# A reordered recurrence, a split output projection, and score rows masked by GpSimd in a two-block model kernel on one NeuronCore

## Time and profile before

| | us |
|---|---|
| median of 3 runs | 3749.43 (3748.31 to 3749.6) |
| profiled execution, its own time | 3750.95 |
| its span, first to last instruction | 3749.2 |
| PE busy | 3447.2 (92%) |
| POOL busy | 2500.9 (67%) |
| DVE busy | 1557.5 (42%) |
| ACT busy | 1491.3 (40%) |
| granted TensorE clock, mean | 0.941 of full speed |

### The profile page before, as it was taken

The page is one execution under the profiler, slowest core; times in us unless marked ns, Lnnn a source line. Parts: engine busy times, 40 slices in busy tenths (PEclk is TensorE's granted clock), DMA queues, the critical chain, the costliest instruction groups (busy, mean ns, idle before and its releaser), DMA issues.

```text
span 3749.2 us, 74946 instructions
## 1 busy us (share of the span) xinstructions
PE 3447.2 (92%) x29214; PEld 3340.4 (89%) x29214; DVE 1557.5 (42%) x2495; ACT 1491.3 (40%) x1968; POOL 2500.9 (67%) x1079
## 2 busy tenths in 40 slices
PE   7898878698999999978769899999999999999999
PEld 7877767598999999978659899999999999999999
DVE  1068543503222210046990158566660266116600
ACT  4345522234444433344333445434344333433333
POOL 5654510086888878855327678777778877877787
PEclk9988877699999999998879999999999999999999
DMA  5843310054556555543215455555556555555555
GB/s 175 187 131 105 102 34 2 24 170 145 181 183 182 182 168 185 185 131 120 83 57 158 143 159 180 168 168 157 171 164 186 175 173 166 182 176 172 171 168 168
DMA packets 158554, 556.41 MB, mean 148 GB/s; under 512 B 17457, under 2 KB 23793, under 8 KB 158305
## 3 DMA queue, kind: packets, MB, share of 16 engines
q1 hardware_dynamic: 151008, 540.08, 46.6%
q0 software_dynamic: 2704, 9.25, 1.4%
q10 hardware_dynamic: 4720, 5.36, 0.5%
HBM read 549.38 MB, written 5.24 MB: 148 GB/s over the span
## 4 chain that ended last, share of the span: by engine, by line
PE 80%; DVE 13%; issue 3%; ACT 2%; POOL 1%; DMA 1%; ACTq 0%; POOLq 0%; DVEq 0%; SPq 0%
PE ps L503 71%; DVE arena L1571 3%; PE ps L688 2%; PE ps L559 1%; PE ps L859 1%; POOL wl L447 1%; DVE arena L1347 1%; PE ps L520 1%; DVE arena L1540 1%; DVE arena L1344 1%; DMA raw<-w_qkv 1%; DVE misc L1538 1%; PE ps L713 1%; PE ps L714 1%; DVE arena L1433 0%
## 5 line engine op out<-in xcount | busy, mean ns | idle before, releaser
L447 POOL TENSOR_TENSOR wl<-raw,wh 128x1024 fp32r<-128x1024 f32 (+1 forms) x1034 | 2477.7, 2401 | 1142.8 <-ACT wh L933 1142.2
L933 ACT ACTIVATE wh<-raw 128x1024 fp32r<-128x1024 f32 (+1 forms) x1034 | 1086.8, 1053 | 1757.8 <-PE ps L503 1696.6
L503 PE MATMUL ps<-uh,wh 128*128 128x256 f32 x5584 | 1614.2, 289 | 83.5 <-DVE ul L1263 43.9
L503 PE MATMUL ps<-ul,wh 128*128 128x256 f32 x5584 | 1600.9, 287 | 0.0
L503 PE MATMUL ps<-uh,wl 128*128 128x256 f32 x5584 | 1598.9, 286 | 0.0
L503 PEld LDWEIGHTS ps<-uh,wh 128*128 128x128 f32 x5584 | 1093.8, 196 | 97.8 <-DVE ul L1263 45.5
L503 PEld LDWEIGHTS ps<-ul,wh 128*128 128x128 f32 x5584 | 1093.0, 196 | 0.4
L503 PEld LDWEIGHTS ps<-uh,wl 128*128 128x128 f32 x5584 | 1093.0, 196 | 0.0
L503 PE MATMUL ps<-el,wh 128*128 128x256 f32 x2048 | 577.5, 282 | 0.0
L503 PE MATMUL ps<-eh,wh 128*128 128x256 f32 x1536 | 439.3, 286 | 9.2 <-DVE el L1706 5.6
L503 PE MATMUL ps<-eh,wl 128*128 128x256 f32 x1536 | 430.3, 280 | 0.0
(11 more groups left out here) (313 smaller groups left out, 3165.0 us busy)
## 6 DMA issues: line engine op xcount, KB each, us to landing
raw<-w_u SPq DMA_DIRECT2D x256, 512.0 KB, 3.6
raw<-w_v SPq DMA_DIRECT2D x256, 512.0 KB, 3.6
raw<-w_gu SPq DMA_DIRECT2D x176, 512.0 KB, 3.6
raw<-w_down SPq DMA_DIRECT2D x80, 512.0 KB, 3.7
raw<-w_out SPq DMA_DIRECT2D x64, 512.0 KB, 3.7
raw<-w_z SPq DMA_DIRECT2D x54, 512.0 KB, 3.6
raw<-w_in SPq DMA_DIRECT2D x52, 512.0 KB, 3.6
raw<-w_qkv SPq DMA_DIRECT2D x48, 512.0 KB, 3.7
```

The lines of the kernel that those rows point to most:

```text
L447: pool.tensor_tensor(wl[:, slot, 0:width], raw[:, slot, 0:width], wh[:, slot, 0:width].bitcast(F32), ALU.subtract).then_inc(lo_ready, 1)
L503: ins = pe.matmul(out, w[:, slot, at], x(c), start=first and c == n == 0, stop=last and c == kt - 1 and n == 2)
L933: act.activation(wh[:, slot, 0:width], raw[:, slot, 0:width], ACT.Copy).then_inc(hi_ready, 1)
```

## The change

- z stage: ScalarE writes `(1 - mix) * z` straight to the destination, and VectorE adds `mix` times the PSUM tile shifted by one step, in place. `zraw`, `zdif` and the subtraction go; a bank is free once VectorE has read it.
- Recurrence: ScalarE copies the lower score rows from PSUM to QS, GpSimd multiplies them by the mask in SBUF. The state's part of y comes right after the right-hand side, the new state before u's part of y; waits are later and split.
- Output projection: first 16 units with the attention half as input, between the group-norm matmuls, each added to xT by `add_attention`; then 16 units with the other half. x is read in four DMAs in place of one. The mean of tile i comes ahead of unit MEAN_AT[i], and the variance of tile i-1 behind it.
- Convolution: the sums of even and odd taps are kept in PSUM bank 7.

`group_mean(i)` and `group_var(i)` hold the former mean and variance matmuls with the same waits.

```diff
+MEAN_AT = (0, 2, 3, 5, 6, 8, 10, 11)
+LAST_VAR_AT = 13
+HALF_BANKS = (2, 3, 6, 7)
...
-        zraw = view(arena, o, 2, T + 1); o += 2 * (T + 1)
-        zdif = view(arena, o, T); o += T
-        sc = view(arena, o, 12, T); o += 12 * T
+        RK = view(arena, o, 2, 2, T); o += 4 * T
+        sc = view(arena, o, 10, T); o += 10 * T
...
+        keep = small[:, 64:91]
+        def z_out(c):
+            i = c // 3 - 1
+            return lo[:, c, :] if c < 3 else vT[:, i, :] if c % 3 == 2 else RK[:, i % 2, c % 3, :]
...
-        odd_taps = qsc[:, 2, :]
+        even_taps, odd_taps = ps[:, 7, 0:T], ps[:, 7, T:2 * T]
...
+            def stream_half(name, dram, half):
+                base = BASE[name] + DT * half
+                with sp.Fori(0, DT // RING) as i:
+                    for j in range(RING):
+                        slot = (base + j) % RING
+                        sp.wait_ge(lo_ready, i * RING + (base + j - RING + 1))
+                        sp.dma_start(raw[:, slot, :],
+                                     dram[bass.ds(i * (2 * RING) + (2 * j + half), 1), :, :]
+                                     .rearrange("a p n -> p (a n)")).then_inc(w_in[slot], 16)
...
+                elif name == "out":
+                    stream_half(name, A["w_out"], 0)
+                    stream_half(name, A["w_out"], 1)
...
-            splits(BASE["out"], 32 + 176)
+            splits(BASE["out"], RING)
+            pool.wait_ge(lo_ready, BASE["out"] + RING)
+            for c in range(NC_):
+                for e in range(2):
+                    pool.wait_ge(low_copied, 2 * c + e + 1)
+                    part = QS.rearrange("p (k e) n -> p e k n", e=2)[CH:P, e, :, :]
+                    mask = cst("cmask")[CH:P].unsqueeze(1).to_broadcast([CH, 8, P])
+                    pool.tensor_tensor(part, part, mask, ALU.mult).then_inc(c_pool, 1)
+            pool.wait_ge(c_pool, 2 * NC_)
+            splits(BASE["out"] + RING, 32 - RING + 176)
...
-                        pe.wait_ge(z_raw, c - 1)
+                        pe.wait_ge(z_ready, c - 1)
...
+                for i in range(WT):
+                    ins = pe.transpose(bank(i // 4)[:, (i % 4) * P:(i % 4 + 1) * P], BK[:, i, c, :], ident)
+                ins.then_inc(bk_tr, 1)
                 if c:
-                    pe.wait_ge(y_ev, c)
-                    pe.wait_ge(st_ev, c)
-                for i in range(WT):
-                    pe.transpose(bank(i // 4)[:, (i % 4) * P:(i % 4 + 1) * P], BK[:, i, c, :], ident)
+                    pe.wait_ge(st_read, c)
...
                 for e in range(2):
                     hp = HD * e
+                    if c and e:
+                        pe.wait_ge(y_ev, c)
                     for k in range(8):
                         ins = pe.matmul(bank(4 + 2 * e + k // 4)[:, (k % 4) * P:(k % 4 + 1) * P],
                                         BK[hp:hp + HD, k, c, :], AR[hp:hp + HD, k, c, :], start=True, stop=True)
@@ -675,6 +712,7 @@
                 for n, step in enumerate(INVERSE):
                     if n == 0:
                         pe.wait_ge(c_dve, c + 1)
+                        pe.wait_ge(low_copied, 2 * c + 2)
...
+                if c:
+                    pe.wait_ge(st_ev, c)
+                pe.wait_ge(c_pool, 2 * c + 2)
...
+                y_out = lambda h: bank(6)[HD * (h % 2):HD * (h % 2) + HD, h // 2 * CH:(h // 2 + 1) * CH]
+                for h in range(NH):
+                    pe.matmul(y_out(h), SV[:, h, :], QS[:, h, CH:P], start=h < 2, stop=False, skip_group_check=True)
...
-                for g in range(GROUPS):
-                    pe.wait_ge(uv_ev, GROUPS * c + g + 1)
-                    for h in range(8 * g, 8 * g + 8):
-                        hp, k = HD * (h % 2), h // 2
-                        out = bank(6)[hp:hp + HD, k * CH:(k + 1) * CH]
-                        pe.matmul(out, SV[:, h, :], QS[:, h, CH:P], start=True, stop=False)
-                        ins = pe.matmul(out, UV[0:CH, h, :], MB[0:CH, h, CH:P], start=False, stop=True)
-                ins.then_inc(y_ps, 1)
+                pe.wait_ge(uv_ev, GROUPS * (c + 1))
                 for h in range(NH) if c < NC_ - 1 else ():
                     ins = pe.matmul(bank(2 + h // 8)[0:CH, (h % 8) * CH:(h % 8 + 1) * CH], BKn[:, h, :],
                                     UV[:, h, :], start=True, stop=True)
                 if c < NC_ - 1:
                     ins.then_inc(n_ps, 1)
-            for i in range(WT):
+                for h in range(NH):
+                    ins = pe.matmul(y_out(h), UV[0:CH, h, :], MB[0:CH, h, CH:P], start=False, stop=h >= NH - 2,
+                                    skip_group_check=True)
+                ins.then_inc(y_ps, 1)
...
-                if i:
-                    pe.wait_ge(gn_sq, i)
...
+            def group_var(i):
+                pe.wait_ge(gn_sq, i + 1)
+                if i >= 2:
+                    pe.wait_ge(gn_rc, i - 1)
+                pe.matmul(bank(4 + i % 2)[:, 0:T], blk, sc[:, i % 2, :], start=True, stop=True).then_inc(gn_var, 1)
+            for d in range(DT):
+                if d in MEAN_AT:
+                    i = MEAN_AT.index(d)
+                    group_mean(i)
+                    if i:
+                        group_var(i - 1)
+                if d == LAST_VAR_AT:
+                    group_var(WT - 1)
+                if d == 0:
+                    pe.wait_ge(ml_ready, 2)
+                if d >= len(HALF_BANKS):
+                    pe.wait_ge(res_attn, d - len(HALF_BANKS) + 1)
+                g = BASE["out"] + d
+                unit(bank(HALF_BANKS[d % 4])[:, 0:T], g + 1, g % RING, uhc, ulc).then_inc(w_used, 1)
+            pe.wait_ge(ml_ready, 2 + WT)
+            for d in range(DT):
+                if d >= 2:
+                    pe.wait_ge(res_ready, d - 1)
+                g = BASE["out"] + DT + d
+                unit(bank(d % 2)[:, 0:T], g + 1, g % RING, lambda c: uh[:, WT + c, :], lambda c: ul[:, WT + c, :])\
+                    .then_inc(w_used, 1)
...
-                    if c >= 2:
-                        act.wait_ge(z_ready, c - 1)
-                    else:
+                    if c == 0:
                         act.wait_ge(z_pad, 1)
-                    act.activation(zraw[:, c % 2, 1:T + 1], bank(c % 2)[:, 0:T], ACT.Copy).then_inc(z_raw, 1)
+                    if c >= 9 and c % 3 == 0:
+                        act.wait_ge(bo_used, c // 3 - 2)
+                    act.activation(z_out(c), bank(c % 2)[:, 0:T], ACT.Identity, scale=keep[:, c:c + 1])\
+                        .then_inc(z_raw, 1)
...
-                act.wait_ge(c_tr, c + 1)
+                act.wait_ge(bk_tr, c + 1)
...
+                for e in range(2):
+                    act.wait_ge(c_ps, 3 * c + e + 1)
+                    for b in range(2):
+                        src = bank(4 + 2 * e + b).rearrange("p (k n) -> p k n", k=4)
+                        ins = act.activation(QS4[CH:P, e, 4 * b:4 * b + 4, :], src[CH:P], ACT.Copy)
+                    ins.then_inc(low_copied, 1)
...
+                if c == NC_ - 1:
+                    act.wait_ge(v_ps, GROUPS * NC_)
+                    for k in (0, 4):
+                        act.activation(uh[:, k:k + 4, :], attnT[:, k:k + 4, :], ACT.Copy).then_inc(mh_ready, 1)
...
-            act.dma_start(xT[:, :, :], x_in).then_inc(s_x2, 16)
-            for c in (0, 4):
-                act.activation(uh[:, c:c + 4, :], attnT[:, c:c + 4, :], ACT.Copy).then_inc(mh_ready, 1)
+            for k in range(4):
+                act.dma_start(xT[:, 4 * k:4 * k + 4, :], x_in[:, 4 * k:4 * k + 4, :]).then_inc(s_x[k], 16)
...
+                for d in range(MEAN_AT[i], MEAN_AT[i + 1] if i + 1 < WT else LAST_VAR_AT):
+                    convert(BASE["out"] + d + RING)
             round_mixed(WT - 1)
-            for c in range(DT):
-                ahead(BASE["out"] + 2 * c)
+            for d in range(LAST_VAR_AT, 2 * DT):
+                convert(BASE["out"] + d + RING)
...
-            dve.memset(zraw[:, :, 0:1], 0.0).then_inc(z_pad, 1)
...
+            dve.tensor_scalar(keep, par[:, PAR["mix"][0]:PAR["mix"][0] + 27], -1.0, 1.0, ALU.mult, ALU.add)\
+                .then_inc(z_pad, 1)
...
-                    if c:
-                        dve.wait_ge(z_ready, c)
-                    z = zraw[:, c % 2, 1:T + 1]
-                    link(dve.tensor_tensor(zdif, zraw[:, c % 2, 0:T], z, ALU.subtract))
-                    i = c // 3 - 1
-                    dst = lo[:, c, :] if c < 3 else (sc[:, 0, :], sc[:, 1, :], vT[:, i, :])[c % 3]
-                    dve.scalar_tensor_tensor(out=dst, in0=zdif, scalar=prm("mix", c), in1=z, op0=ALU.mult, op1=ALU.add)\
-                        .then_inc(z_ready, 1)
+                    late = z_out(c)[:, 1:T]
+                    dve.scalar_tensor_tensor(out=late, in0=bank(c % 2)[:, 0:T - 1], scalar=prm("mix", c), in1=late,
+                                             op0=ALU.mult, op1=ALU.add).then_inc(z_ready, 1)
...
```

(34 more changed lines are left out.)

38 lines of the change are left out of this document (15 added, 23 removed).

## The result

The kernel with the change takes 3692.25 us (median of 4 runs, 3687.30 to 3694.73), the kernel before, run beside it, 3748.87 (3745.54 to 3749.60). The ratio is 0.985, with a 95% interval from 0.9834 to 0.9865: 1.5% faster. The profiled execution took 3691.38 for a span of 3689.6, at a granted clock of 0.949 (before 0.941). The forecast of 3698 lies 6 above it. It will turn out that the total was right by luck: three terms that were too small cancelled one with the wrong sign.

What follows compares the result with a forecast made beforehand. TensorE holds 80% of the chain, but in the changed stretches it waits for others, and VectorE waits for GpSimd's splits; savings of 8 + 32 + 3 + 8 = 51 from 3749.4 give 3698 us, own range 3682 to 3714.

Steps and rivals of the forecast that it cites:

- The z stage: Mix from PSUM slips past GpSimd's splits, later operations inherit part of the wait: 8 us saved, bounds 3 and 20.
- the four times 0.8: Late z iterations 17, 20, 23 and 26: L1298 can start 0.8 earlier, when the split ends; 3.3 us in all.
- The recurrence: Shorter chain from u's copies to the next inverse, and shorter last chunk: 32 us saved, bounds 24 and 45.
- Rival (4): Recurrence: y's matmuls stay slow in any order, 5.0 a block; 29 us lost, 3727; chance 0.06.
- My 1.6 for u's part: Recurrence: u's part of y takes 1.6 us, between 1.15 (L697) and 3.6 (L717).
- The projection: Units beside group norm: 3 us saved where sixteen hidden units promise 46; bounds 12 saved to 16 lost.
- rival (1): Group norm: each VectorE remainder waits for GpSimd's splits, 26.4 us, some 22 on the path; 3720; chance 0.22.
- the forecast 9.1: Group norm: serial iterations 3, 5, 6 and 7 take 9.1 us each: VectorE iteration, unit, mean and variance, adds.
- The convolution: With sums in PSUM, taps no longer wait for splits: 8 us saved, bounds 0 and 12 without the tap's price.
- The other waits, at L1538 and L1540, stay: Convolution: VectorE's waits for splits at these operations remain, apart from 2 us by which L1538 is released earlier.
- Rival (3): Convolution: PSUM taps are slow, 0.73 each; 248 taps cost 82 us more, kernel slower at 3788; chance 0.05.
- Rival (2): z stage: waits vanish if L1287 gets in ahead of the split pair; nine iterations lose 4.3 each, 3660; chance 0.08.

Runs made afterwards that it cites:

- e3: The changed kernel with the z stage of the kernel before (copy to SBUF, subtraction, mix of two SBUF tensors): 3702.74 us, 10.5 slower.
- e8: The changed kernel with only y's 64 matmuls alternating per head between state's part and u's part, as before: 3737.25 us, 45.0 slower.
- e4: The changed kernel with the lower score rows' masks back on VectorE from PSUM, without ScalarE's copies and GpSimd's masks: 3689.27 us.
- e1: The changed kernel with group norm and output projection as in the kernel before (whole tiles after the group norm): 3671.22 us, ratio 0.9792.
- e5: The changed kernel with the remainders of the group norm's output computed by GpSimd between its splits, not by VectorE: 3681.67 us, ratio 0.9828.
- e6: The changed kernel with each add of an attention unit one VectorE iteration earlier, remainders still on VectorE: 3665.43 us, ratio 0.9778.
- e2: The changed kernel with the sums of the convolution's taps back in SBUF: 3706.93 us, 14.7 slower.

## Why the prediction was right, and where it wasn't

The total was right to 6 us, and that was luck: three of the four terms lie beyond their bounds, two as gains and one as a loss, so that +6.5, +16.6, -22.2 and +6.8 came to 7.7.

**The z stage: 8 forecast, 10.5 (e3) to 14.5 (the two traces) measured, within 3 and 20.** The mechanism held: mixes at 0.48, the wait inherited by L1354. Against the operation's times before, the early iterations (up to 12) gained 4.7 in all, as forecast (3.5 + 1). The late ones gained more than the four times 0.8: 3.8 between iterations 12 and 15, where one old subtraction had stood 10.16, and 6.0 behind it. I had read one late iteration and multiplied.

**The recurrence: 32 forecast, 48.6 measured, beyond the bound of 45.** The step that failed is the price of TensorE's blocks: state 3.6, turns 3.6 and products 7.4 were taken from rows of a chunk whose granted clock was 0.50 there; in after's chunk, with no alternating block ahead, they took 2.0, 1.9 and 3.4. Two windows of TensorE's work, before and after:

```profile
604.00:615.00 11.00, 10.86 (x64) 10.00 (x66) 4.70 (x7) 4.27 (x5) 0.00 (x0) 0.50 0.01 1
```

```profile
524.00:535.00 11.00, 9.95 (x160) 9.34 (x158) 6.73 (x12) 5.09 (x8) 0.11 (x1) 1.00 0.01 1
```

I had weighed a higher clock for the products alone (a gain of 9.4) and took 8.5; the mean gain in the distance of y's copies was 14.9. Ahead of the fall stood the alternating block in the kernel before and in e8. Rival (4), y slow in any order, is out: its blocks take 1.1. My 1.6 for u's part, "as the output halves still alternate", was too much by 0.5. GpSimd's masks were priced well in kind (L1445 waits 3.1 where 2.2 was forecast), and e4 shows that they gain nothing. The first chunk, put at 0, lost 1.6: from the last bonus product to the inverse are 16.8, before 15.2. Here the clock went the other way: the first products took 6.4 at a granted 0.50 (490.5 to 498.5), before 3.8 at 0.91 (503.5 to 508.5), though no alternating block stands ahead of them in either kernel. So the block's order is not all that the level hangs on, and what else it is stays open.

**The projection: 3 saved forecast, 19.2 lost by the traces and 21 by e1, beyond the bound of 16 lost.** This was rival (1), at 0.22, and its price of 22 on the path came out almost to the digit: -3 + 22 = 19. That is luck too: its own terms, three waits of 2.4 and five of 4.8, make 31.2 and not 26.4, and only about half of the loss is its wait. A long iteration is the forecast 9.1, 2.15 of wait and 2.2 of a slower unit, 13.4 by this estimate, where 12.5 to 13.7 were measured. What failed is the step that ruled it out, "the sixth tap starts at 1811.5, 0.1 after the split's record, and isn't delayed". In after L1509 starts at 678.82, 0.09 behind the record of the pair (678.73), and waits; L1504 starts 0.06 behind one (658.72 and 658.66) and takes 2.58. One tap, whose own start was interpolated in a row of six, had outweighed a rule. The Trainium skill (SBUF — State Buffer, "Who interferes with whom") says that a VectorE operation with two SBUF inputs contends with GpSimd's reads and that whoever issues first keeps the port pair for the whole instruction. These rows agree with it; but in the earlier trace rows L1347 starts 0.20 ahead of the pair's record and waits as well, so a recorded start alone doesn't tell who is first. The forecast of "a pair (4.8) in five" iterations is off: beside a pair L1509 waited for one split, 2.6, and got in between the two. What stood in for it is the unit at 1.2 GHz, 5.1 instead of 2.89, after TensorE had idled for 5.11. e5 and e6 part the loss: taking the remainder off VectorE returned 10.6 by the times and 4.7 by the trace, taking the adds out of the serial chain 26.8 and 32.2.

**The convolution: 8 forecast, 14.8 by the traces and 14.7 by e2, beyond the 12.** The tap's price (unchanged) and the blocked taps (100.7 to 94.9, so 5.8 of 6.3) were right. "The other waits, at L1538 and L1540, stay" was wrong: these operations with L1541 fell from 63.7 to 53.0. The two that open the sums, which the sum left out, cost 2.1 more. Rival (3) is out.

Rival (2) is out too: L1354 waits in all of the iterations 0 to 12, with 3.75 to 4.25 us in eleven of them and 1.84 and 3.34 in the two others.

## What to carry to other kernels

A sum that comes out right doesn't prove its terms: check each at its own points in both traces, since here an edit that lost 19 hid behind others that gained 78 (48.6 + 14.5 + 14.8). A duration is worth taking only with the clock level of its row, and an edit can change that level for what stands behind it, either way: up behind the reordered y, down in the first chunk. One trace doesn't price an edit to 3 us: compare the stages that it doesn't touch, too (e5's trace held 11.2 that were not its own). When engines are interleaved to hide work, write down the cycle of waits of one iteration: moving the adds by one iteration was worth 27 us, more than taking one wait out of each.

## What was not expected of the hardware

Single-precision matmuls of 64 columns that follow each other at 0.034 us (32 in 1.09) begin 0.13 apart when each pair changes between 128 and 64 rows into the same sum (0.26 for two), and the granted clock fell from its upper to its lower level within such a block (its 11.9 would be 32 x 0.26 = 8.3 at the upper one), though TensorE issued without a gap. GpSimd's mask of 64 partitions x 1024 values takes 2.35, as long as the split of 128 partitions x 1024 (2.40): half the partitions save nothing. Beside a pair of splits in the group norm a `tensor_tensor` of VectorE waited for one of them (2.58), and in the z stage a `tensor_scalar` for both (4.13 of 4.65). The form isn't the reason: in the z stage before, the `tensor_tensor` L1344 waited for both of a pair (5.51, at 320.19) and for four splits in a row (10.16, at 357.03). When VectorE gets in between two splits isn't shown.
